# Items of the down projection split into high and low parts two at a time, with twelve raw slots

## The reference, cut to what matters

```python
D_MODEL, SEQ, D_FF = 1024, 512, 2816

def swiglu_ffn(x, w_gate, w_up, w_down):
    h = silu(einsum('bsd,df->bsf', x, w_gate)) * einsum('bsd,df->bsf', x, w_up)
    return einsum('bsf,fd->bsd', h, w_down)          # the down projection

ff = swiglu_ffn(h, w_gate, w_up, w_down)
out = layer_norm(DEEPNORM_ALPHA * h + ff, ln2_g, ln2_b)
```

## Time and profile before

| | us |
|---|---|
| median of 3 runs | 718.79 |
| the profiled execution | 718.96 |
| its span, first to last instruction | 717.2 |
| PE busy | 694.5 (97%) |
| DVE busy | 438.7 (61%) |
| ACT busy | 338.5 (47%) |
| POOL busy | 183.7 (26%) |
| DVE waiting for ACT at `al`, 560 to 718 us | 17.6 |

### The profile page before, as it was taken

One profiled execution on the slowest core, in us unless ns is written; L12 is line 12 of the kernel. 1 busy time (PEld: TensorE's weight loads), 2 busy tenths in 40 slices (PEclk: granted clock), 3 DMA queues, 4 the chain that ended last, 5 costly groups with the idle time before them and its releaser, 6 DMA issues.

```text
span 717.2 us, 9505 instructions
## 1 busy us (share of the span) xinstructions
PE 694.5 (97%) x3380; PEld 580.6 (81%) x3380; DVE 438.7 (61%) x703; ACT 338.5 (47%) x627; POOL 183.7 (26%) x166
## 2 busy tenths in 40 slices
PE   8998999999999999999899999999999999999965
PEld 6987887888888888888798888888888888888844
DVE  5669999767876236635934434443333348888886
ACT  6677787467766354422442222222222234677641
POOL 2112221000001000002744656455533317000112
PEclk9999999999999999999999999999999999999989
DMA  8121112221113523341056666665466523677542
GB/s 326 65 90 59 59 59 84 83 69 60 59 59 129 223 89 103 103 158 49 30 184 233 228 211 239 225 241 196 174 207 206 174 88 104 202 217 202 172 127 108
DMA packets 34723, 102.09 MB, mean 142 GB/s; under 512 B 3584, under 2 KB 3712, under 8 KB 34688
## 3 DMA queue, kind: packets, MB, share of 16 engines
q1 hardware_dynamic: 27504, 74.36, 31.2%
q0 software_dynamic: 7184, 27.27, 11.3%
HBM read 87.99 MB, written 13.63 MB: 142 GB/s over the span
## 4 chain that ended last, share of the span: by engine, by line
PE 68%; DVE 19%; DMA 5%; ACT 3%; issue 2%; POOL 2%; SPq 0%; DVEq 0%; POOLq 0%; ACTq 0%
PE ps L1369 20%; PE ps L1371 20%; PE ps L1370 20%; DVE sl L883 3%; DMA raw<-in_wdn 3%; DVE prob L1055 2%; DVE al L883 2%; DMA raw<-tw 2%; PE ps L1449 2%; DVE smax L1035 1%; PE ps L1435 1%; ACT rope L615 1%; ACT sh L852 1%; DVE ptl L883 1%; POOL rstd L518 1%
## 5 line engine op out<-in xcount | busy, mean ns | idle before, releaser
L883 DVE TENSOR_TENSOR sl<-raw,sh 128x512 fp32r<-128x512 f32 (+1 forms) x113 | 117.5, 1040 | 74.0 <-ACT sh L833 74.0
L1369 PE MATMUL ps<-hTh,sh 128*128 128x512 f32 (+1 forms) x384 | 143.6, 374 | 2.7 <-DVE hTl L883 2.7
L1370 PE MATMUL ps<-hTh,sl 128*128 128x512 f32 (+1 forms) x384 | 143.3, 373 | 0.0
L1371 PE MATMUL ps<-hTl,sh 128*128 128x512 f32 (+1 forms) x384 | 143.3, 373 | 0.0
L833 ACT ACTIVATE sh<-raw 128x1024 fp32r<-128x1024 f32 x36 | 38.2, 1062 | 148.3 <-PE ps L1371 139.3
L1369 PE MATMUL ps<-xh,sh 128*128 128x512 f32 x224 | 90.8, 406 | 0.4 <-DVE xl L1189 0.4
L879 DVE TENSOR_TENSOR sl<-raw,sh 128x1024 fp32r<-128x1024 f32 x44 | 54.7, 1243 | 55.3 <-ACT sh L603 55.2
L1371 PE MATMUL ps<-xl,sh 128*128 128x512 f32 x224 | 87.9, 392 | 0.0
L1370 PE MATMUL ps<-xh,sl 128*128 128x512 f32 x224 | 87.6, 391 | 0.0
L1369 PEld LDWEIGHTS ps<-hTh,sh 128*128 128x128 f32 x384 | 73.0, 190 | 15.6 <-DVE hTl L883 3.1
L1370 PEld LDWEIGHTS ps<-hTh,sl 128*128 128x128 f32 x384 | 73.1, 190 | 12.5
(11 more groups left out here) (206 smaller groups left out, 1235.9 us busy)
## 6 DMA issues: line engine op xcount, KB each, us to landing
raw<-in_slabs SPq DMA_DIRECT2D x87, 512.0 KB, 3.3
stage<-in_wdn POOLq DMA_DIRECT2D x11, 1024.0 KB, 9.1
tw<-tsum POOLq DMA_DIRECT2D x11, 1024.0 KB, 5.6
raw<-tw SPq DMA_DIRECT2D x44, 256.0 KB, 2.8
raw<-in_wdn SPq DMA_DIRECT2D x33, 256.0 KB, 3.0
x_raw<-in_xT SPq DMA_DIRECT2D x8, 256.0 KB, 5.1
res<-in_x POOLq DMA_DIRECT2D x1, 2048.0 KB, 8.8
out<-res SPq DMA_DIRECT2D x8, 256.0 KB, 2.9
```

Of the source, the lines that this page charges most:

```text
L883: return dve.tensor_tensor(dst, src, hi.bitcast(F32), ALU.subtract)
L1369: pe.matmul(dst, lh, rh, start=start, stop=False)
L1370: pe.matmul(dst, ll, rh, start=False, stop=False)
L1371: return pe.matmul(dst, lh, rl, start=False, stop=stop)
```

## The change

DN_RAW goes from 4 to 12. Slots 0 to 3 stay in `raw`; slots 4 to 11 are a new tile `dn_raw`, 8 x 512 values per partition, at 32 KB: the place of `hTh`. Loads of e = 4 to 11 wait for `slab_done` of N_DN, that is until all gate and up matmuls are done; later ones for item_ready of e - 12. ACT and DVE handle items 2k and 2k + 1 together. Ring waits of both items come first (`part_free`), then one Copy of both activation parts (128 x 512), or two if the items belong to different products (e = 10 and 11, 32 and 33, 54 and 55), then the landing of both weight tiles, then one Copy of both (128 x 1024). DVE's lo goes the same way. Both counters rise by two at the end of a pair. The 77th item goes alone. The steps between items keep their place in the loop; where such a step follows an even item, that item's odd neighbour is now parted ahead of it.

```diff
-DN_RAW = 4
+DN_RAW = 12
+DN_EARLY = 4
...
+        dn_raw = at("dn_raw", 32, [P, (DN_RAW - DN_EARLY) * 512])
...
+        def item_raw(e, count=1):
+            r = e % DN_RAW
+            if r < DN_EARLY:
+                return raw[:, r * 512:(r + count) * 512]
+            return dn_raw[:, (r - DN_EARLY) * 512:(r - DN_EARLY + count) * 512]
...
+        def item_parts(e):
+            p, i = divmod(e, PAIRS)
+            return parts[:, i:i + 2, PRODUCTS[p][0] * 2 * P:(PRODUCTS[p][0] + 1) * 2 * P]
...
-                if e < DN_RAW:
+                if e < DN_EARLY:
                     sp.wait_ge(lo_ready, N_DN - 1 + e // 2)
+                elif e < DN_RAW:
+                    sp.wait_ge(slab_done, N_DN)
                 else:
                     sp.wait_ge(item_ready, e - DN_RAW + 1)
...
             def item_split(e):
+                s = e % RING
+                if e + 1 < ITEMS and one_product(e):
+                    part_free(e, e + 2)
+                    act.activation(ah[:, s:s + 2, :], item_parts(e), ACT.Copy)
+                else:
+                    part_free(e, e + 1)
+                    act.activation(ah[:, s, :], item_part(e), ACT.Copy)
+                    if e + 1 < ITEMS:
+                        part_free(e + 1, e + 2)
+                        act.activation(ah[:, s + 1, :], item_part(e + 1), ACT.Copy)
+                count = min(2, ITEMS - e)
+                for m in range(e, e + count):
+                    act.wait_ge(item_landed[m % DN_RAW], 16 * (m // DN_RAW + 1))
+                act.activation(item_slot(sh, e, count), item_raw(e, count), ACT.Copy).then_inc(item_hi, count)
...
                 item_split(2 * r)
-                item_split(2 * r + 1)
             for e in range(RING, ITEMS):
-                item_split(e)
+                if e % 2 == 0:
+                    item_split(e)
...
             def item_low(e):
-                dve.wait_ge(item_hi, e + 1)
-                low(al[:, e % RING, :], item_part(e), ah[:, e % RING, :])
-                low(item_slot(sl, e), item_raw(e), item_slot(sh, e)).then_inc(item_ready, 1)
+                s = e % RING
+                count = min(2, ITEMS - e)
+                dve.wait_ge(item_hi, e + count)
+                if count == 2 and one_product(e):
+                    low(al[:, s:s + 2, :], item_parts(e), ah[:, s:s + 2, :])
+                else:
+                    for m in range(e, e + count):
+                        low(al[:, m % RING, :], item_part(m), ah[:, m % RING, :])
+                low(item_slot(sl, e, count), item_raw(e, count), item_slot(sh, e, count)).then_inc(item_ready, count)
...
                 item_low(2 * r)
-                item_low(2 * r + 1)
             left = None
             for e in range(RING, ITEMS):
-                item_low(e)
+                if e % 2 == 0:
+                    item_low(e)
```

More of the change, by code:

```diff
@@ L389, in item_part, with item_slot, one_product @@
             return parts[:, i, PRODUCTS[p][0] * 2 * P:(PRODUCTS[p][0] + 1) * 2 * P]
[L391 to L395, removed]
+        def item_raw(e, count=1):
[3 more added lines that the diff above has]
+            return dn_raw[:, (r - DN_EARLY) * 512:(r - DN_EARLY + count) * 512]
+        def item_slot(ring, e, count=1):
+            return ring[:, item_offset(e):item_offset(e) + 512 * count]
+        def item_parts(e):
+            p, i = divmod(e, PAIRS)
+            return parts[:, i:i + 2, PRODUCTS[p][0] * 2 * P:(PRODUCTS[p][0] + 1) * 2 * P]
+        def one_product(e):
+            return e // PAIRS == (e + 1) // PAIRS
         block = ctx.enter_context(nc.Block())
@@ L833, in _, with part_free @@
                     act.activation(slot(sh, m), raw_of(m), ACT.Copy).then_inc(hi_ready, 1)
-            def item_split(e):
[L837 to L847, removed]
-                else:
[L849 to L852, removed]
+            def part_free(e, end):
+                for e in range(e, end):
+                    p, i = divmod(e, PAIRS)
+                    if e == 0:
+                        act.wait_ge(t_stored, 16 * PAIRS)
+                    if p == M5:
+                        act.wait_ge(part_made, 3 * i + 1)
+                    if e == M1 * PAIRS:
+                        act.wait_ge(part_made, 3 * PAIRS)
+                    if p == M3:
+                        act.wait_ge(s3_made, i + 1)
+                    if e < RING:
+                        act.wait_ge(slab_done, N_DN - SPL + 1 + e // 2)
+                    else:
+                        act.wait_ge(item_done, e - RING + 1)
```

## The result

| | before | after |
|---|---|---|
| median of 9 runs each, us | 718.19 | 721.86 |
| lowest and highest | 717.13, 719.31 | 720.17, 724.23 |
| the profiled execution | 718.96 | 721.86 |
| its span | 717.2 | 720.1 |

The ratio is 1.0053, with a 95% interval of 1.0036 to 1.0071: the change makes the kernel slower by 2.6 to 5.1 us. The forecast was 720.8. The median of the kernel before is not the same in every set of runs: 718.19 here, 718.9 in the 31 runs beside the first experiments.

What follows compares the result with a forecast made beforehand. PE was taken to bound the kernel, its one loss a 6.4 us gap at M4 plus 2.5 us of half clock. Terms 1.5 + 1.6 - 1.1 = +2.0 us gave 720.8 us, range 717.2 to 723.2.

Steps and rivals of the forecast that it cites:

- case A: The forecast itself, all terms summed: +2.0 us, 720.8 us, own spread 719.3 to 722.5; chance 0.57.
- the 0.3 for item 65: Before the gap at M4: 0.3 us lost because item 65 was parted only just when wanted; expected to go.
- Loads of items 4 to 11: Before item 4: loads issued late, item 5 landing at 599.1, stall PE 1.5 us, bounds 0.9 and 2.8.
- What waits behind it: Behind item 4, delayed silu(21) and POOL additions slow DVE, holding PE at pairs: 1.6 us lost, bounds 0 and 4.
- Merged instructions: On DVE, 1.74 us a pair for 1.88, saving 0.14; all beside PE except in the end chain.
- The end chain: Steps up to the take of M7's block 0: M4 starts 0.8 us earlier; recorded gain 1.1, bounds 0.3 and 3.6.
- Twelve slots: ACT's waits of 0.2 to 1.8 us on loads go, but PE's work covers them; priced 0.
- B: At the gap before M4, PE keeps 2.4 GHz: 2.5 us less, 718.3; chance 0.14.
- C: The take of M7's block 0 comes early: 6.1 us less than before, 712.7 at full; chance 0.12.
- E: Loads interleave, so item 5 lands only when all twelve have, about 606.9: 728 us; chance 0.07.
- D: Only the first stall, before item 4, costs time; DVE and POOL don't collide as counted: 719.2 us; chance 0.10.

Runs made afterwards that it cites:

- e1: The changed kernel with loads of items 4 to 7 back in the four old slots, issued early; 718.05 us.
- e3: The changed kernel with pairs undone, ACT and DVE taking single items; twelve slots and late loads kept; 722.22 us.
- e8: The changed kernel with POOL's eleven S3 additions cut to one column each; 719.51 us, only its time means anything.
- e2: The changed kernel with silu(21) on ACT and hidden(21) on DVE ahead of items 4 and 5, loads still late; 721.09 us.
- e6: The kernel before, single items and four slots, with only the order behind M7 altered so the take of its block 0 comes early; 712.84 us.
- e9: e5 with single items instead of pairs: twelve slots, early loads of items 4 to 7, early take of M7's block 0; 711.66 us.
- e5: The changed kernel with early loads of items 4 to 7 and M7's block 0 taken right after items 66 and 67; 711.17 us, again 710.93.

## Why the prediction was right, point by point

- **Direction and size**: forecast +2.0 us with case A; the profiled executions differ by 2.9, the medians by 3.7 (2.6 to 5.1). The cause is that of case A, as e1 shows by taking it away. The 0.8 us between profiles and medians is no term of the forecast: the median of the kernel before moves by 0.7 from set to set, and F and the half clock by more (last section).
- **The sum has a slip.** The chain gives M4's start as 690.95 instead of 691.73, which is 0.8 us. That already holds the 0.3 for item 65, since the end of the gap is set by DVE and not by when PE got there (0.3, and 0.5 of gap: 6.4 to 5.9). The 0.3 was added once more, to 1.1. By its own terms the sum is 1.5 + 1.6 - 0.8 = +2.3 us.
- **Loads of items 4 to 11**: forecast item 5 landed at 599.1, lo done 602.0, PE at 602.2. Measured 599.05, 601.97, 602.03. The wait was 1.3 us, forecast 1.5.
- **What waits behind it**: forecast 1.6 us by the walk (pairs ready at 604.9, 607.75, 611.25), measured 1.6 (start waits 2.9 less 1.3), with item 10 at 611.18 where 611.35 was forecast, and 2.83 us a pair for 2.82. e3 and e8 show that POOL's work is in it; e2 that its place is not.
- **Merged instructions**: a DVE pair free of POOL takes 1.73 us (622.52 to 624.25 in the changed kernel), the 1.74 taken from start-to-start rows. The Trainium skill's fixed latency for each instruction (VectorE: DVE Perf Modes, The TRN2 errata) gives the single durations well, but by it a pair would have saved 0.31 us; it saved 0.15. The measurement decides: the next instruction hides the rest.
- **The end chain is the step that failed in size.** Forecast: a gain of 0.8 us (recorded as 1.1). Measured: 0.2, that is the 0.3 for item 65, which is not owed to pairs (e1, e3), less 0.1 for a gap of 6.5 and not 5.9. The statistics started on time (678.31, forecast 675.3 + 3.1 = 678.4). Scale then came 0.25 us late: L535 took 1.81 us beside the pair's lo, 0.27 when alone, which the forecast had only as its lower bound. The steps behind it followed late, and by the last take the sum was 0.5 us (693.73, forecast 690.15 + 3.1 = 693.25). DVE waited 1.46 us for ACT before items 68 and 69, before 0.82: a pair in two wide steps gives DVE nothing to start on while ACT works.
- **Twelve slots priced 0**: near enough for the change: e1 is not measurably faster than before with them, and the most that the profiles give them is the 0.3 us at item 65. Once nothing else is late they are worth 1.2 us, in one profile each of e6 and e9.
- **Rivals**: B did not happen, twelve matmuls ran at half clock (694.56 to 699.81). C, the early take, did not come of itself; of its price, put at 9.2 us, e5 got 7.8 from F to T; 0.4 us at M4 and 1.0 behind it are what was left. E fell: the twelve loads landed in order, item 4's 2.6 us after its issue, item 5's 3.0, the last 6.4 (priced 728; 7.8 us later than A would be 728.6). D fell: 1.6 us of waits stand behind the first stall.

## What to carry to other kernels

Where a buffer is enlarged into space that becomes free only at a stage's end, ask which loads had been issued ahead of that end, and leave those their old slots: four of 77 loads cost 2.9 us here, and giving them back cost nothing. A lead over the bounding engine matters most where another engine's work will slow the one that prepares (here 0.54 us for each DVE instruction beside POOL's additions); lost there, it wasn't regained for 20 us. And before widening a pipeline, see which instruction ended PE's longest gap: it was one take written too late in DVE's order, and moving it alone was worth 5 us (e6), pairs and slots together 1.8 more (e5).

## What the runs showed that was not expected

**The time ahead of the down projection varies.** F lies at 595.3 us in the profiles of before and after, at 593.5 to 594.0 in e1, e6, e8 and e9, and at 596.4 in the first of e5, with code ahead of it that the edits don't touch. Busy time from 330 to 360 us, around the first layer norm, of e1, of after, and of e5's first profile, with the granted clock third from the end:

```profile
330.00:360.00 30.00, 27.32 (x164) 23.97 (x163) 26.97 (x43) 11.01 (x18) 20.36 (x22) 1.00 0.06 21
```

```profile
330.00:360.00 30.00, 27.31 (x151) 23.94 (x150) 26.16 (x43) 10.90 (x18) 19.22 (x20) 0.94 0.06 20
```

```profile
330.00:360.00 30.00, 27.33 (x141) 23.99 (x140) 25.68 (x42) 10.26 (x18) 18.16 (x19) 0.89 0.06 18
```

PE is busy for the same 27.3 us of the 30 in all three; behind its idleness of some 2.5 us between 345 and 355 us the clock falls, or doesn't (from 350 to 355 us it is 1.00, 0.68 and 0.55), and F follows: 593.79, 595.39, 596.42. That is up to 2.6 us between executions of the same code there, as large as the effect studied.

**The same behind the gap at M4.** Behind a gap of 6.5 us each, M4 to T is 2.6 us over the 15.2 of full clock in after (17.8), 2.1 in e1 (17.3), 1.4 and 1.5 in e8 and e2 (16.6, 16.7). Why the half clock ends earlier in some isn't settled here. A difference of 1 us between two kernels that both have the gap can be this alone.

**POOL's small instructions beside DVE.** L535 works on one column and takes 0.27 us; beside a run of DVE's instructions it took 1.81 and ended about when they did. The wide S3 additions take turns with DVE instead, one for one. What makes the difference was not tried.
